# Mixer A, heads 0 to 4: 15 of 20 probability tiles transposed by VectorE in 32x32 blocks and by transfers within SBUF instead of by TensorE

## The chip, the core and the metric

The kernel is one program on one core of a Trainium2 chip. The metric is the device time in microseconds, from launch to the last write. The kernel before takes 865.27 us, the median of 3 runs (863.59 to 866.17).

## The reference

One layer of a bidirectional encoder, x of 512 tokens by 1024, float32:

```python
h = rms_norm(x)
z = h @ w_in                      # q, k, v of mixer A; q, k, v of mixer B; two gates
ya = axial_gqa_attention(qa, ka, va) @ w_o_a
yb = dilated_window_attention(qb, kb, vb) @ w_o_b
x = x + (gate_a * ya + gate_b * yb) @ w_out
x = x + expert_choice_swiglu(rms_norm(x))     # 16 experts, 64 tokens each
return rms_norm(x)
```

Mixer A has 8 query heads of 64 and 2 key heads. Per head and query block it computes s = q k^T over all 512 keys, p = softmax(s), o = p v. The change touches the way in which p gets its keys onto the partitions, so that p v can be summed over them.

## The kernel before, in words

Tokens are dealt to 4 tiles of 128: token 4 i + c lies on partition i of tile c. The kernel runs in stages on one core: norm and token-major projections; mixer A (8 heads of 4 query tiles, 32 tiles u = 4 head + c); mixer B (4 heads, 16 tiles); gates, branch projections and output projection; router; then 8 pairs of experts, whose weights stream from HBM. Each engine has its own instruction list, written out by hand, and semaphores join them. There is no planner: the order in which each engine makes its steps is the order of the loops below, and an engine that waits holds up all that stands behind it in its list.

In mixer A the lists run in turns u:

- TensorE (`for u in range(NA)`, lines 1391 on): `scores_a(u + 2)` makes two 128x512 score matmuls (L1322) into one of three PSUM banks and waits for `exp_done` of tile u-1, whose bank it takes; `values_a(i)` (L1364), at u = 9, 17 and 25 and once in mixer B, sums p v of two heads in 16 matmuls; `fill` makes one or two steps of three matmuls (L1165 to L1167) of the projections of mixer B, by the plan `A_FILL`; `turn_probs(u)` makes four 128x128 transposes (L1352) of the normalised probabilities of tile u into PSUM.
- VectorE (`for u in range(NA + 5)`): the maximum of tile u (L2010); `norm_probs(u - 1)`, a reciprocal (L1980) and a scaling of 128x512 (L1982); `low_col`, the low parts of finished q and k columns of mixer B (L1998, L2002, L2003), `split_lo` (L1887), the low part of a weight strip, in the turns `A_LOWS`; `low_o`, the low part of a pair's output, in the turns `O_LOW`.
- ScalarE (`for u in range(NA + 4)`): `soft_exp(u)` (L885), `read_probs(u - 2)` (L897), the copy of the transposed tile from PSUM into `pT`, `high_col` (L916, L919, L920), `split_hi` (L801), `read_o` in the turns `O_READ`. From head 2 on `read_probs` waits for `pv_done`, since it overwrites the `pT` that `values_a` reads.
- SyncE issues the loads of the weight strips, one DMA each, in the order of `strips`. `load_strip(n)` (L595) waits until VectorE has split strip n-4. Strips 12 to 23 are the q and k columns of mixer B.

`pT` holds two heads, `[key partition, head % 2, key tile, query]`. The probabilities lie in three rotating buffers `probs_a`; `wait_probs_free` holds an exponential until the tile three before has been transposed.

```python
for u in range(NA):
    if u + 2 < NA:
        scores_a(u + 2)
    if u > 1 and u % (2 * NT) == 1:
        values_a(u // (2 * NT) - 1)
    fill(A_FILL, u, cols_a, A_LEAD)
    turn_probs(u)
```

## Time and profile before

| | |
|---|---|
| median of 3 runs | 865.27 us (863.59 to 866.17) |
| profiled execution | span 862.3 us from the first to the last instruction; no time of its own is listed for it beside the three |
| instructions | 10445 |
| TensorE busy | 843.6 us, 98% |
| VectorE, ScalarE, GpSimd busy | 373.8, 264.2, 29.1 us |
| HBM | 235.92 MB read, 2.62 MB written |
| granted TensorE clock | 0.996 of full speed, mean |

The profile is one execution. PE is TensorE's matmul, PEld its weight load, DVE is VectorE, ACT ScalarE, POOL GpSimd, SP SyncE. L1352 is line 1352 of the kernel. Durations of neighbours on one engine overlap, so what an instruction costs is read from the distance of starts. The chain is the work that ended last, followed back from the end at each step to what released it.

### The profile page before, as it was taken

To read this page: it belongs to the slowest core of one execution; us is meant where nothing else is said; L and a number is where in the kernel's file an instruction comes from. 1 tells how busy PE (TensorE), PEld (TensorE's weight loads), DVE (VectorE), ACT (ScalarE), POOL (GpSimd) and SP (SyncE) were. 2 spreads that over 40 slices of the span, in tenths; PEclk is the share of its full clock that TensorE was granted. 3 is DMA by queue.
4 is the path that set the end of the run, shared out by engine and by line. 5 is a ranking of instruction groups with operands and counts; after the bars stand their busy time and mean duration, and the time that the engine had idled before them with its cause. 6 is when DMAs were issued, how large, how long until landed. Compare 5 with 4: busy or idle time off the path is not lost.

```text
span 862.3 us, 10445 instructions
## 1 busy us (share of the span) xinstructions
PE 843.6 (98%) x4229; PEld 517.8 (60%) x4229; DVE 373.8 (43%) x648; ACT 264.2 (31%) x461; POOL 29.1 (3%) x50
## 2 busy tenths in 40 slices
PE   9999999999999999999999999999999998989996
PEld 8898866787878888888534343344433433334343
DVE  6377987776616244427322236223131321312351
ACT  6333876685624233216011010010100101001231
POOL 1050000000000000003000000000000000000010
PEclk9999999999999999999999999999999999999999
DMA  9730112033034334884899999999999999999996
GB/s 286 177 98 2 49 49 98 25 87 97 20 122 134 92 92 143 310 369 165 333 406 424 427 431 427 427 426 429 426 427 428 428 428 427 427 424 429 425 421 256
DMA packets 81491, 239.20 MB, mean 277 GB/s; under 512 B 8102, under 2 KB 63526, under 8 KB 65828
## 3 DMA queue, kind: packets, MB, share of 16 engines
q1 hardware_dynamic: 76016, 235.94, 69.4%
q10 hardware_dynamic: 5284, 2.09, 1.0%
q8 instruction: 34, 0.56, 0.3%
q0 software_dynamic: 144, 0.51, 0.1%
q14 instruction: 13, 0.11, 0.0%
HBM read 235.92 MB, written 2.62 MB: 277 GB/s over the span
## 4 chain that ended last, share of the span: by engine, by line
PE 90%; DMA 8%; DVE 1%; issue 0%; ACT 0%; POOLq 0%; POOL 0%; SPq 0%; DVEq 0%; ACTq 0%
PE psum L1652 21%; PE psum L1165 11%; PE psum L1684 11%; PE psum L1166 11%; PE psum L1167 11%; DMA wslot<-in_w_down 8%; PE psum L1609 3%; PE psum L1703 3%; PE psum L1352 3%; PE psum L1813 2%; PE psum L1322 2%; PE psum L1364 2%; PE psum L1338 2%; PE psum L1171 1%; PE psum L1664 1%; PE psum L1617 1%
## 5 line engine op out<-in xcount | busy, mean ns | idle before, releaser
L1652 PE MATMUL psum<-wslot,xinT 128*64 128x512 f32 x1000 | 222.3, 595 | 4.6 <-DMA wslot<-in_w_up 2.8
L1652 PEld LDWEIGHTS psum<-wslot,xinT 128*64 128x64 f32 x1000 | 69.3, 137 | 142.7 <-issue 131.3
L1684 PE MATMUL psum<-wslot,actT 128*64 128x512 f32 x424 | 95.8, 596 | 3.8 <-DMA wslot<-in_w_down 3.8
L1165 PE MATMUL psum<-hT_hi,w_hi 128*128 128x512 f32 x208 | 82.9, 399 | 0.0
L1167 PE MATMUL psum<-hT_hi,w_lo 128*128 128x512 f32 x208 | 81.2, 390 | 0.0
L1166 PE MATMUL psum<-hT_lo,w_hi 128*128 128x512 f32 x208 | 81.2, 390 | 0.0
L1887 DVE TENSOR_TENSOR w_lo<-w_raw,w_hi 128x1024 fp32r<-128x1024 f32 (+1 forms) x46 | 52.9, 1175 | 44.9 <-ACT w_hi L801 44.7
L1684 PEld LDWEIGHTS psum<-wslot,actT 128*64 128x64 f32 x424 | 29.4, 137 | 59.8 <-issue 57.3
L1097 ACT ACTIVATE actT<-psum 128x512 f32<-128x512 f32 x16 | 9.6, 598 | 171.7 <-PE psum L1664 171.7
L2294 DVE TENSOR_TENSOR x<-x,psum 128x512 f32<-128x512 f32 x48 | 29.8, 682 | 57.5 <-PE psum L1703 57.5
L2284 DVE TENSOR_TENSOR y_lo<-psum,y_hi 64x512 fp32r<-64x512 f32 x28 | 19.3, 689 | 79.7 <-ACT y_hi L1107 79.3
L801 ACT ACTIVATE w_hi<-w_raw 128x1024 fp32r<-128x1024 f32 (+1 forms) x46 | 45.2, 1017 | 16.3 <-PE psum L1167 16.3
L1165 PEld LDWEIGHTS psum<-hT_hi,w_hi 128*128 128x128 f32 x208 | 39.1, 188 | 10.0 <-issue 2.6
L1167 PEld LDWEIGHTS psum<-hT_hi,w_lo 128*128 128x128 f32 x208 | 39.0, 188 | 8.4
L1166 PEld LDWEIGHTS psum<-hT_lo,w_hi 128*128 128x128 f32 x208 | 39.1, 188 | 7.5
L1092 ACT ACTIVATE act<-psum,slot_vals 128x512 f32<-128x512 f32 x16 | 11.0, 687 | 93.3 <-PE psum L1652 93.3
L2271 DVE SCALAR_TENSOR_TENSOR act<-psum,slot_vals,act 128x512 f32<-128x512 f32 x16 | 12.0, 750 | 59.1 <-ACT act L1092 59.0
L897 ACT ACTIVATE pT<-psum 128x512 f32<-128x512 f32 x48 | 28.5, 595 | 22.7 <-PE psum L1352 13.3
L1107 ACT ACTIVATE y_hi<-psum 64x512 fp32r<-64x512 f32 x28 | 16.5, 589 | 57.3 <-PE psum L1684 57.0
L1609 PE MATMUL psum<-xn,pick 128*128 128x512 f32 x120 | 29.4, 396 | 0.0
L2237 DVE TENSOR_TENSOR xinT<-psum,small 128x512 f32<-128x512 f32 x15 | 9.7, 686 | 40.0 <-PE psum L1617 40.0
L2277 DVE SCALAR_TENSOR_TENSOR act<-act,slot_fac,psum 128x512 f32<-128x512 f32 x16 | 12.0, 748 | 31.9 <-PE psum L1652 31.9
(281 smaller groups left out, 1307.7 us busy)
## 6 DMA issues: line engine op xcount, KB each, us to landing
wslot<-in_w_up SPq DMA_DIRECT2D x24, 2048.0 KB, 25.5
wslot<-in_w_gate SPq DMA_DIRECT2D x24, 2048.0 KB, 24.5
wslot<-in_w_down SPq DMA_DIRECT2D x22, 2048.0 KB, 22.5
w_raw<-in_w_in SPq DMA_DIRECT2D x34, 512.0 KB, 4.6
wslot<-in_w_up SPq DMA_DIRECT2D x15, 1024.0 KB, 10.5
wslot<-in_w_down SPq DMA_DIRECT2D x15, 1024.0 KB, 27.6
wslot<-in_w_gate SPq DMA_DIRECT2D x14, 1024.0 KB, 11.2
w_raw<-in_w_out SPq DMA_DIRECT2D x8, 512.0 KB, 4.7
```

The lines of the kernel that those rows point to most:

```text
L801: act_.activation(hi, raw, ACT.Copy).then_inc(w_hi_done, 1)
L897: last = act_.activation(pT[:, head % 2, :, cols], tp[(0, 3)[u % 2]][:, :].rearrange("p (k i) -> p k i", i=P), ACT.Copy)
L1165: pe.matmul(out_, s_hi, m_hi, start=(k == 0), stop=False)
L1166: pe.matmul(out_, s_hi, m_lo, start=False, stop=False)
L1167: return pe.matmul(out_, s_lo, m_hi, start=False, stop=(k == n_k - 1))
L1352: t = pe.transpose(tp[(0, 3)[u % 2]][:, P * k:P * k + P], probs_of(u)[:, P * k:P * k + P], ident[:, :])
L1609: mm = pe.matmul(bank[6 + f][:, :], pick[:, c, :, :], part[:, c, cols], start=(c == 0 and part is xn_hi), stop=(c == NT - 1 and part is xn ...
L1652: mm = pe.matmul(bank[2 * e + n][CAP * f:CAP * f + CAP, :], xinT[:, HALF * h + k, CAP * e:CAP * e + CAP], wslot[place_of(m)][:, k % PART, ...
L1684: mm = pe.matmul(bank[4 + e][CAP * f:CAP * f + CAP, :], actT[:, e, k, CAP * h:CAP * h + CAP], wslot[place_of(m)][:, k % PART, SEQ * f:SEQ ...
L1703: mm = pe.matmul(bank[added_bank(c, f)][:, :], give[:, p % 2, P * c:P * c + P], part[:, SEQ * f:SEQ * f + SEQ], start=(part is y_hi), stop ...
L1887: dve.tensor_tensor(lo, raw, hi.bitcast(F32), ALU.subtract).then_inc(w_split, 1)
L2294: dve.tensor_tensor(part, part, bank[added_bank(c, f)][:, :], ALU.add).then_inc(added, 1)
```

## The change

For the tiles c = 0, 1, 2 of heads 0 to 4 (`in_blocks`, 15 of the 32 tiles of mixer A) the way of the probabilities is another one:

- VectorE makes the reciprocal alone; ScalarE scales the 128x512 tile in place (`scale_probs`); VectorE transposes it in sixteen 32x32 blocks (`turn_blocks`) into one of two buffers `blocks`; when the three tiles of a head are there, SyncE issues 16 DMAs of 32 partitions by 4 by 96 numbers from `blocks` into `pT` (`move_blocks`), which carries each block to the partitions of its keys. TensorE's four transposes and ScalarE's copy out of PSUM are left out for these tiles.
- Tile c = 3 of each of these heads, and all tiles of heads 5 to 7, go as before. `whole_before(u)` counts those.
- `move_blocks(0)` to `move_blocks(4)` stand on SyncE ahead of the loads of strips 19 to 23. From head 2 on they wait for `pv_done`. A buffer of `blocks` is written again once its head has been moved.
- `values_a(0)` to `values_a(2)` stand in turns 12, 20 and 25, with `read_o` and `low_o` behind them, and wait for the transfers of their heads too.
- In `pT` the queries of heads 0 to 5 lie in another order, which `read_o` and `low_o` put right with strided patterns.
- Two pairs of load semaphores are joined into `shape_parts_in`. `high_col` waits for head 3's transfer ahead of the k column of group 1, whose place one `blocks` buffer shares.

```diff
@@ -55,6 +55,8 @@
+SQ = 32
+BLOCK_HEADS = 5
 COL_A = 0
@@ -123,6 +125,7 @@
     pT = sb("pT", [2, NT, SEQ], W0)
+    blocks = [sb(f"blocks{i}", [NT, NT, 3 * SQ], kib) for i, kib in enumerate((96, W0 + 76))]
     probs_a = [sb(f"probs_a{i}", [SEQ], W0 + 16 + 2 * i) for i in range(3)]
@@ -387,11 +392,44 @@
+        def in_blocks(u):
+            return u < NT * BLOCK_HEADS and u % NT < NT - 1
+        def whole_before(u):
+            return sum(not in_blocks(v) for v in range(u))
+        def blocks_before(u):
+            return u - whole_before(u)
+        def wait_blocks_in(eng, h):
+            eng.wait_ge(blocks_in[h % 2], 16 * NT * NT * (h // 2 + 1))
         def wait_probs_free(eng, u):
             before = u - 3 if u < NA else max(u - 3, NA - 1)
-            if before >= 0:
-                eng.wait_ge(probs_turned, before + 1)
+            if before >= 0 and in_blocks(before):
+                eng.wait_ge(blocks_turned, blocks_before(before + 1))
+            elif before >= 0:
+                eng.wait_ge(probs_turned, whole_before(before + 1))
+        def turned_bank(u):
+            return tp[(0, 3)[whole_before(u) % 2]]
+        def token_order(i, rows):
+            if i > (BLOCK_HEADS - 1) // 2:
+                return rows
+            return rows.rearrange("p (q c s) -> p c q s", q=NT, c=NT)
+        def by_tiles(i, rows):
+            if i > (BLOCK_HEADS - 1) // 2:
+                return rows
+            return rows.rearrange("p (c q s) -> p c q s", q=NT, c=NT)
@@ -471,7 +509,8 @@
         A_FILL = [min(N_COL_A * KC, A_LEAD + 2 + (i + 1) * (N_COL_A * KC - A_LEAD - 2) // (NA - 1)) for i in range(NA)]
-        O_READ, O_LOW = (10, 19, 26), (11, 21, NA)
+        VALUES_AT = (12, 20, 25)
+        O_READ, O_LOW = (14, 22, 26), (15, 23, NA)
         A_LOWS = (5, 7, 10, 16, 20, 26)
@@ -639,8 +678,21 @@
+            def move_blocks(h):
+                sp.wait_ge(blocks_turned, 3 * (h + 1))
+                if h >= 2:
+                    sp.wait_ge(pv_done, h // 2)
+                for kq in range(NT):
+                    for q in range(NT):
+                        sp.dma_start(pT[SQ * kq:SQ * kq + SQ, h % 2, :, P * q:P * q + 3 * SQ],
+                                     blocks[h % 2][SQ * q:SQ * q + SQ, :, kq, :]).then_inc(blocks_in[h % 2], 16)
             load_x(0)
             for n in range(len(strips)):
+                if 19 <= n < 19 + BLOCK_HEADS:
+                    move_blocks(n - 19)
                 load_strip(n)
@@ -893,17 +945,28 @@
                     act_.wait_ge(pv_done, head // 2)
-                act_.wait_ge(probs_turned, u + 1)
-                last = act_.activation(pT[:, head % 2, :, cols],
-                                       tp[(0, 3)[u % 2]][:, :].rearrange("p (k i) -> p k i", i=P), ACT.Copy)
+                act_.wait_ge(probs_turned, whole_before(u + 1))
+                if head <= (BLOCK_HEADS - 1) // 2 * 2 + 1:
+                    dst = pT[:, head % 2, :, :].rearrange("p k (q c s) -> p k q c s", q=NT, c=NT)[:, :, :, c, :]
+                    src = turned_bank(u)[:, :].rearrange("p (k q s) -> p k q s", k=NT, q=NT)
+                else:
+                    dst = pT[:, head % 2, :, cols]
+                    src = turned_bank(u)[:, :].rearrange("p (k i) -> p k i", i=P)
+                last = act_.activation(dst, src, ACT.Copy)
                 if u >= NA:
...
+            def scale_probs(u):
+                act_.wait_ge(probs_normed, u + 1)
+                p = probs_of(u)[:, 0:SEQ]
+                act_.activation(p, p, ACT.Copy, scale=column(rinv, u)).then_inc(probs_scaled, 1)
             def read_o(i):
                 act_.wait_ge(pv_done, i + 1)
-                act_.activation(oT_hi[:, i, :], tp[2][:, :], ACT.Copy).then_inc(o_hi_done, 1)
+                act_.activation(by_tiles(i, oT_hi[:, i, :]), token_order(i, tp[2][:, :]), ACT.Copy).then_inc(o_hi_done, 1)
@@ -916,6 +979,8 @@
                 else:
+                    if (grp, hp, hh) == (1, 0, 0):
+                        wait_blocks_in(act_, BLOCK_HEADS // 2 * 2 - 1)
                     act_.activation(kB[half, hh, grp, 0, :], src[half, :], ACT.Copy)
@@ -925,8 +990,10 @@
-                        act_.dma_start(dist[:, :, :], distance).then_inc(dist_in, 16)
-                if 2 <= u < NA + 2:
+                        act_.dma_start(dist[:, :, :], distance).then_inc(shape_parts_in, 16)
+                if u and in_blocks(u - 1):
+                    scale_probs(u - 1)
+                if 2 <= u < NA + 2 and not in_blocks(u - 2):
                     read_probs(u - 2)
@@ -1339,23 +1406,27 @@
             def turn_probs(u):
+                if in_blocks(u):
+                    return
                 pe.wait_ge(probs_normed, u + 1)
...
-                    pe.wait_ge(pT_done, u)
+                    pe.wait_ge(pT_done, whole_before(u))
                     for g in range(2):
...
                                      probs_of(u)[:, SEQ + P * g:SEQ + P * g + P], ident[:, :])
-                elif u >= 2:
-                    pe.wait_ge(pT_done, u - 1)
+                elif whole_before(u) >= 2:
+                    pe.wait_ge(pT_done, whole_before(u) - 1)
                 for k in range(NT):
-                    t = pe.transpose(tp[(0, 3)[u % 2]][:, P * k:P * k + P],
+                    t = pe.transpose(turned_bank(u)[:, P * k:P * k + P],
                                      probs_of(u)[:, P * k:P * k + P], ident[:, :])
...
-                pe.wait_ge(pT_done, 2 * NT * (i + 1))
+                pe.wait_ge(pT_done, whole_before(2 * NT * (i + 1)))
+                for h in range(2 * i, min(2 * i + 2, BLOCK_HEADS)):
+                    wait_blocks_in(pe, h)
                 if i:
@@ -1391,8 +1462,8 @@
                     scores_a(u + 2)
-                if u > 1 and u % (2 * NT) == 1:
-                    values_a(u // (2 * NT) - 1)
+                if u in VALUES_AT:
+                    values_a(VALUES_AT.index(u))
                 fill(A_FILL, u, cols_a, A_LEAD)
@@ -1977,14 +2048,27 @@
                 dve.wait_ge(exp_done, u + 1)
+                if in_blocks(u):
+                    dve.reciprocal(column(rinv, u), column(rsum, u)).then_inc(probs_normed, 1)
+                    return
                 settle(dve.reciprocal(column(rinv, u), column(rsum, u)))
...
+            def turn_blocks(u):
+                head, c = divmod(u, NT)
+                if c == 0 and head >= 2:
+                    wait_blocks_in(dve, head - 2)
+                dve.wait_ge(probs_scaled, blocks_before(u + 1))
+                dve.transpose(blocks[head % 2][:, :, :, SQ * c:SQ * c + SQ].rearrange("p k q s -> p (k q) s"),
+                              probs_of(u)[:, 0:SEQ].rearrange("p (b s) -> p b s", s=SQ)).then_inc(blocks_turned, 1)
             def low_o(i):
                 dve.wait_ge(o_hi_done, i + 1)
-                dve.tensor_tensor(oT_lo[:, i, :], tp[2][:, :], oT_hi[:, i, :].bitcast(F32), ALU.subtract)\
-                    .then_inc(o_lo_done, 1)
+                dve.tensor_tensor(by_tiles(i, oT_lo[:, i, :]), token_order(i, tp[2][:, :]),
+                                  by_tiles(i, oT_hi[:, i, :].bitcast(F32)), ALU.subtract).then_inc(o_lo_done, 1)
@@ -2011,6 +2095,8 @@
                     norm_probs(u - 1, SEQ)
+                if u >= 2 and in_blocks(u - 2):
+                    turn_blocks(u - 2)
                 for g in range(N_COL_A):
```

## Rows read from the trace of the kernel before

**Rows 1.** Page part 1: busy time, share of the span and instructions of each engine.

```profile
PE 843.6 (98%) x4229; PEld 517.8 (60%) x4229; DVE 373.8 (43%) x648; ACT 264.2 (31%) x461; POOL 29.1 (3%) x50
```

**Rows 2.** Page part 4: the chain that ended last, shares by engine.

```profile
PE 90%; DMA 8%; DVE 1%; issue 0%; ACT 0%; POOLq 0%; POOL 0%; SPq 0%; DVEq 0%; ACTq 0%
```

**Rows 3.** Stretches: length, busy time of each engine, TensorE clock, DMA share, GB/s.

```profile
88.00:111.20 23.20, 23.20 (x121) 16.92 (x119) 21.75 (x43) 17.80 (x38) 0.00 (x0) 1.00 0.16 46
111.20:163.00 51.80, 51.77 (x269) 37.80 (x268) 39.98 (x83) 38.46 (x83) 0.00 (x0) 1.00 0.22 72
500.00:600.00 100.00, 100.00 (x471) 41.69 (x471) 36.94 (x59) 10.75 (x18) 0.00 (x0) 1.00 1.01 428
```

**Rows 4.** The chain in order of time: start, length, what.

```profile
107.93 3.58 PE psum L1364 x16
...
116.99 0.44 PE psum L1352 x4
117.43 0.46 PE psum L1322 x2
```

**Rows 5.** Groups by line and form, ScalarE, 88 to 163 us.

```profile
L897 ACT ACTIVATE pT<-psum 128x512 f32<-128x512 f32 x30 | 17.8, 593 | 10.8 <-PE psum L1364 9.4 <-PE psum L1352 1.4
```

**Rows 6.** Waits, 88 to 163 us: total, times, longest.

```profile
ACT pT L897 <- PE psum L1364: 9.4, 3, 3.6
...
DVE kB L2002 <- ACT kB L920: 4.5, 3, 3.6
```

**Rows 7.** VectorE in order of time: start, duration, line, operation.

```profile
98.81 1.22 DVE L1887 TENSOR_TENSOR w_lo<-w_raw,w_hi 128x1024 fp32r<-128x1024 f32 x1
99.94 0.68 DVE L2010 TENSOR_REDUCE small<-psum 128x1 f32<-128x512 f32 x1
100.54 0.15 DVE L1980 RECIPROCAL small<-small 128x1 f32<-128x1 f32 x1
100.73 0.49 DVE L1982 TENSOR_SCALAR probs_a<-probs_a,small 128x512 f32<-128x512 f32 x1
101.13 0.68 DVE L2010 TENSOR_REDUCE small<-psum 128x1 f32<-128x512 f32 x1
...
109.96 0.68 DVE L2010 TENSOR_REDUCE small<-psum 128x1 f32<-128x512 f32 x1
```

**Rows 8.** SyncE's DMA issues in order of time, and line 583's time to landing.

```profile
350.87 1.77 SPq L657 DMA_DIRECT2D x<-in_x  x4
...
401.02 0.68 SPq L628 DMA_DIRECT2D wslot<-in_w_up  x1
...
190.07 0.51 SPq L584 DMA_DIRECT2D w_raw<-in_w_o_b  x1
...
DMA to landing us min/median/max: 2.6/2.7/3.0
```

**Rows 9.** TensorE in order of time: start, duration, line, operation.

```profile
117.73 0.40 PE L1165 MATMUL psum<-hT_hi,w_hi 128*128 128x512 f32 x1
...
119.12 0.60 PE L1352 MATMUL psum<-ident,probs_a 128*128 128x128 f32 x4
...
136.75 0.70 PE L1322 MATMUL psum<-kA,qA 128*128 128x512 f32 x2
137.29 0.40 PE L1165 MATMUL psum<-hT_hi,w_hi 128*128 128x512 f32 x1
...
147.48 3.65 PE L1364 MATMUL psum<-pT,vA 128*64 128x512 f32 x16
```

**Rows 10.** Stretches as in rows 3, at the start and the end.

```profile
5.00:10.00 5.00, 5.00 (x26) 3.53 (x25) 2.85 (x4) 3.43 (x5) 0.77 (x2) 0.90 1.13 349
854.00:855.00 1.00, 0.89 (x3) 0.06 (x1) 0.21 (x1) 0.76 (x3) 0.00 (x0) 1.00 0.08 33
...
858.00:859.00 1.00, 0.00 (x0) 0.00 (x0) 0.00 (x0) 0.00 (x0) 0.72 (x1) 0.94 0.00 0
859.00:862.30 3.30, 0.00 (x0) 0.00 (x0) 0.00 (x0) 0.00 (x0) 0.51 (x1) 0.50 0.38 154
```

More of the change, by code:

```diff
@@ L243, in encoder_block @@
         g1_spread = sem("g1_spread")
-        rope_parts_in = sem("rope_parts_in")
+        shape_parts_in = sem("shape_parts_in")
         gains_in = sem("gains_in")
         x_tile_in = [sem(f"x_tile_in{c}") for c in range(NT)]
-        dist_in = sem("dist_in")
         w_raw_in = [sem(f"w_raw_in{i}") for i in range(RING + 2)]
@@ L274, in encoder_block @@
         probs_turned = sem("probs_turned")
+        probs_scaled = sem("probs_scaled")
+        blocks_turned = sem("blocks_turned")
+        blocks_in = [sem(f"blocks_in{i}") for i in range(2)]
         pT_done = sem("pT_done")
@@ L808, in _ @@
             square_x(2)
-            act_.dma_start(rope_in[:, :, :, :], rope).then_inc(rope_parts_in, 16)
+            act_.dma_start(rope_in[:, :, :, :], rope).then_inc(shape_parts_in, 16)
             for dst, src in ((gq, q_norm_g), (gk, k_norm_g)):
-                act_.dma_start(dst[:, :], src[0].partition_broadcast(P)).then_inc(rope_parts_in, 16)
+                act_.dma_start(dst[:, :], src[0].partition_broadcast(P)).then_inc(shape_parts_in, 16)
             square_x(3)
@@ L1368, in values_b @@
             def values_b(hp):
-                pe.wait_ge(pT_done, NA + 2 * NT * (hp + 1))
+                pe.wait_ge(pT_done, whole_before(NA + 2 * NT * (hp + 1)))
                 pe.wait_ge(o_lo_done, OA + hp)
@@ L1901, in _ @@
                 split_lo(n)
-            dve.wait_ge(rope_parts_in, 16 * 3)
+            dve.wait_ge(shape_parts_in, 16 * 3)
             for n, g in enumerate((gq, gk)):
@@ L2025, in _ @@
                     low_o(O_LOW.index(u))
-            dve.wait_ge(dist_in, 16)
+            dve.wait_ge(shape_parts_in, 16 * 4)
             for hp in range(2):
```

## The prediction

> **What bounds the kernel now.** I read the busy shares first: TensorE (PE) is busy 98% of the 862.3 us span [rows 1]. The chain that ended last lies on it for 90%, with 8% on the weight loads [rows 2]. Two stretches differ by limit. Mixer A is 88 to 163 us: there TensorE is busy throughout, and in its first part VectorE nearly as much (21.75 of 23.2 us), afterwards 39.98 of 51.8; the DMA engines are used for about a fifth. Late, at 500 to 600 us, TensorE and the DMA engines are both full, but the DMA there is fed by slots that TensorE frees [rows 3]. So a microsecond won or lost in mixer A moves everything behind it by one, as long as TensorE is what runs out there.
>
> I call the 32 query tiles of mixer A u = 0 to 31 (head u // 4). In turn u TensorE makes scores(u+2), some projection steps, then the transposes of tile u. VectorE in its turn u takes the maximum of tile u and normalises u-1. scores(u+2) waits for the exponential of u-1.
>
> **TensorE.** Four transposes take 0.44 us on the chain, two score matmuls 0.46, a values_a of 16 matmuls 3.58 [rows 4]. 15 of the 20 tiles of heads 0 to 4 lose their transposes: 15 x 0.44 = 6.6 us less. That is the whole prize. values_a moves from turns 9, 17, 25 to 12, 20, 25.
>
> **ScalarE.** Each of the 15 tiles exchanges a 128x512 copy out of PSUM (593 ns, [rows 5]) for a scaling of 128x512 in SBUF. Between the copy's 593 and a little over that, I take no change. Its wait for values_a (3 times, 9.4 us in all, [rows 6]) moves with values_a and stays as long. The strided reads and writes of read_o and low_o keep their element counts, so nothing is charged; they lie off the chain.
>
> **VectorE.** Starts of neighbours give the pitch: the scaling of 512 numbers 0.40 us (100.73 to 101.13), the maximum over 512 numbers 0.60 (99.94 to 100.54), a 1024-number subtraction 1.13 (98.81 to 99.94) [rows 7]. No row shows a VectorE transpose. I bound it by 0.40 and 1.13 and take 0.60, since it passes 512 numbers once like the maximum. So each of 15 tiles adds 0.2 us, 3.0 in all. In the first part VectorE has no room: seven tiles (0, 1, 2, 4, 5, 6, 8) are turned ahead of max(11), which moves from 109.96 [rows 7] to 111.4. It also waits some 0.8 us at the first tile of head 2 for head 0's transfer to land (110.3, below, against 109.5 wanted). Then 0.6 for the maximum and some 0.7 for the exponential: scores(14) can run at about 113.5 and end at 114.0. TensorE alone would have been there near 110.
>
> **The transfers.** This term decides. Each of five heads is moved by 16 DMAs that SyncE issues one after the other, 80 in all. An issue holds SyncE: four loads in a row with no wait between them took 1.77 us (0.44 each), two others 0.68 (0.34), and one after another took 0.51 alone, so with the gap 0.55 [rows 8]. I take 0.41 per issue, and 0.34 to 0.55 as bounds. The smallest weight loads land 2.7 us after their issue (2.6 to 3.0) [rows 8]; mine are in SBUF at both ends, so 2.0 is possible. A head thus needs 15 x 0.41 + 2.7 = 8.9 us from first issue to landing and blocks SyncE for 6.6.
>
> Order on SyncE: strip 18 waits for a split that ends at 99.94 [rows 7], plus 0.6 for three transposed tiles, so it is issued at 100.65. Head 0 goes 101.1 to 107.6 (landed 110.3), strip 19 to 108.0, head 1's last DMA is issued at 108.0 + 6.15 = 114.2 and lands at 116.9. values_a(0) waits for it, with TensorE standing behind: it starts at 116.9 instead of 114.0 and ends at 120.5. Before, TensorE had reached the same place in the order (values_a(0) made, projection steps of turn 12 next) at 117.73 [rows 9]. So it is 2.8 us late there already.
>
> Heads 2 and 3 overwrite what values_a(0) reads, so SyncE waits for it, then issues 32 DMAs and two strips: 120.5 + 6.6 + 0.4 + 6.15 + 2.7 = 136.3, and values_a(1) can end at 139.9. VectorE gives a second bound for the same place. Tile 19 is still transposed by TensorE, and its normalising stands behind, from max(15) at 120.5 + 1.4 + 0.5 = 122.4: six maxima 3.6, six reciprocals 1.1, four transposes 2.4, two scalings 0.8, one low_o 0.7, one split 1.1, four 64x512 subtractions of the k column 2.8, which is 12.5; and for ScalarE's k copies about 1.5 (such waits cost 4.5 us now, [rows 6]). That makes 136.4, transposes and scores 0.9, values_a(1) 3.6: 140.9. Before, that place was reached at 137.29 [rows 9]. Both paths say late, by 2.6 and 3.6. I take +3.7 with the small SyncE waits.
>
> Head 4 goes after values_a(1): 140.9 + 15 x 0.41 + 2.7 = 149.8. TensorE needs 10.2 us from there to values_a(2) (137.29 to 147.48, [rows 9]), so until 151.1: hidden by 1.3 us, and by less than nothing if an issue costs 0.55. The strips that now stand behind transfers (19 to 23) are needed turns later, the last in mixer B: no cost while the queue is free by 150. ScalarE's wait before the k column of group 1 is for head 3, landed long before. The freed semaphore and the shared count cost nothing.
>
> A rule of the Trainium skill speaks otherwise about the main term. The rows show 0.34 to 0.55 us for one issue [rows 8]. The page "DMA: Bandwidth & Descriptors", section "Anatomy of one DMA — SWDGE (gpsimd) path", puts the sequencer's dispatch of a DMA at about 50 ns; if that held on SyncE here, 16 issues would be an estimated 0.8 us and the transfers would be hidden. That is rival B below; the rows do not bear it out.
>
> **Sum.** -6.6 of TensorE work, +10.3 of waits (the two values_a and tile 19), so +3.7: span 862.3 to 866.0. The profiled execution's span lies 3.0 under the median of 865.27, so on that scale the forecast is 865.3 + 3.7 = 869.0. About 0.3% (2.6 us) is what a measurement of this kernel can tell from no change.
>
> **Rivals.**
> A, the forecast: SyncE's issues and VectorE's chain hold both values_a back. With issues of 0.34 the transfers would allow 135.5, but VectorE's chain, from a values_a(0) ending at 118.3, still 138.7 (+1.4); with 0.55, values_a(1) ends at 113.7 + 64 x 0.55 = 148.9, and head 4 adds 0.8: +12.4. Its own range is 866.7 to 877.7. For it: nothing on SyncE between issues explains the 0.4 but the issue itself. Chance 0.45.
> B, issues are cheap and transfers hidden, VectorE alone limits: values_a(0) starts at 114.0, VectorE's chain then gives 117.6 + 1.9 + 12.5 + 4.5 = 136.5 and up to 1.5 of waiting for ScalarE, so within 1 us of the old 137.29, 865.3. For it: VectorE is at 94% in the first part [rows 3]. Chance 0.22; that the change does nothing to the chain at all is another 0.02 at the same time.
> C, the other side: a VectorE transpose costs about 0.40, the same as the scaling it replaces, and an issue less than 0.33. The transfers let values_a(1) end at 113.7 + 64 x issue, which equals the old 137.29 at 0.37 and is 2.6 better at 0.33; below that VectorE decides: max(11) stays at 109.96, values_a(0) ends at 111.8 + 3.6 = 115.4, then 1.9 + 11.7 + 1.1 and 4.5 as above, 134.6. So -2.7: 862.6, and never better than -6.6, 858.7. Against it: no issue in the trace is under 0.33. Chance 0.16.
> D, A plus the clock. TensorE would stand idle about 3 us before values_a(0) and 3.4 before tile 19's transposes. At the end of the kernel it stops at 854.9, and the granted clock is 0.94 in 858 to 859 and 0.50 after, i.e. 1.2 instead of 2.4 GHz; after an early fall 5 to 10 us shows 0.90 [rows 10]. A fall that lasts as long as the one row of 3.3 us at half clock costs 1.7 us of work; two make 872.4. No row shows an idle of 3 us within the kernel, so it is open. Chance 0.07.
> E, a transpose costs 1.13: VectorE adds 0.5 to each of seven tiles first and four later, the start of values_a(0) moves to 117.7 and the second chain by 2.1, so about +6.5, 871.8. Chance 0.08.
>
> **How the numbers follow.** A, D and E are slower by over 0.3%: 0.60. B and nothing: 0.24. C: 0.16, its time on the edge of 0.3% and beyond. The predicted time is A's, 869.0. The range 862.0 to 878.0 takes in B, the near half of C and A's upper bound; A's own stands above.
>
> **What would show it.** The SyncE rows of the new DMAs: a pitch of 0.4 us makes 6.6 us a head. TensorE's waits: matmuls of values_a released by a DMA, about 3 us for the first, and its start near 117 instead of 107.9. Tile 19's transposes released by VectorE, 3 us idle. The VectorE transpose at 0.6 us pitch (duration about 0.69). values_a(1) ending near 141 against 131.5, and the projection step behind it near 141 against 137.29; mixer B beginning 3.7 us late and everything behind it shifted by the same. Wrong would be: issues of 0.1 us, no idle before values_a, or a shift that is made up before 163 us.

## The result, and the profile after

| | before | after |
|---|---|---|
| median of 4 runs each | 864.43 us (862.91 to 866.17) | 893.50 us (892.86 to 894.07) |
| ratio | | 1.0335, 95% interval 1.0317 to 1.0353 |
| profiled execution | span 862.3 us | 893.24 us, span 891.3 us |
| mean granted TensorE clock | 0.996 | 0.976 |

The kernel is 29 us slower. The forecast was 869.0 us with a range of 862 to 878: the direction was right, the size was not, and it lies outside the range. Some executions of the kernels here, the one before included, take about 2.5 us more than the others, and where a trace shows this it is there before 60 us, ahead of the change.

The page of the changed kernel, its parts 1, 2 and 4. It answers to [rows 1] and [rows 2]:

```profile
PE 846.7 (95%) x4169; PEld 515.5 (58%) x4169; DVE 375.7 (42%) x648; ACT 265.9 (30%) x461; POOL 29.0 (3%) x50
...
PEclk9999967899999999999999999999999999999998
...
PE 82%; DMA 8%; SPq 5%; DVE 2%; issue 2%; ACT 1%; POOLq 0%; POOL 0%; DVEq 0%; ACTq 0%
```

TensorE fell from 98% busy to 95%, and its share of the chain from 90% to 82%. SyncE's queue (SPq), which was not on the chain, holds 5% of it. The granted clock drops in slices 6 to 8 of 40, which is mixer A.

Where the time went is seen by comparing the two kernels at the same places in TensorE's order:

| place in TensorE's order | before | after | later by |
|---|---|---|---|
| projection steps of turn 12, values_a(0) made | 117.73 | 129.66 | 11.9 |
| projection steps of turn 20, values_a(1) made | 137.29 | 159.59 | 22.3 |
| values_a(2) begins, turn 25 | 147.48 | 175.89 | 28.4 |
| mixer B's first scores | 163.15 | 193.31 | 30.2 |
| end of the span | 862.3 | 891.3 | 29.0 |

All of it is lost between 105 and 193 us; 1 us comes back behind, in stages that were not changed. The stretches, answering to [rows 3]; columns are the window, busy us and count of PE, PEld, DVE, ACT and POOL, then the granted clock, the DMA share and GB/s:

```profile
88.00:111.20 23.20, 20.61 (x92) 15.95 (x91) 19.41 (x37) 19.45 (x40) 0.00 (x0) 1.00 0.20 53
111.20:130.00 18.80, 9.25 (x28) 3.92 (x28) 7.64 (x15) 4.50 (x11) 0.00 (x0) 0.64 0.39 104
130.00:150.00 20.00, 14.27 (x60) 10.49 (x58) 15.48 (x28) 14.47 (x29) 0.00 (x0) 0.88 0.39 96
150.00:170.00 20.00, 16.86 (x70) 10.19 (x70) 8.98 (x22) 9.85 (x22) 0.00 (x0) 0.77 0.37 106
170.00:190.00 20.00, 14.11 (x62) 8.95 (x63) 9.48 (x18) 7.23 (x16) 0.00 (x0) 0.83 0.33 75
190.00:210.00 20.00, 20.00 (x120) 15.19 (x120) 14.76 (x34) 14.13 (x30) 0.00 (x0) 1.00 0.00 1
```

From 111 to 130 us TensorE works for half of the time, VectorE for 41% and ScalarE for 24%: nobody is busy, so something outside of the three is waited for. The waits between 88 and 195 us name it (total, times, longest):

```profile
DVE small L2094 <- PE psum L1389: 21.5, 4, 10.3
...
PEld psum L1421 <- DVE probs_a L2056: 13.8, 6, 4.9
PE psum L1421 <- DVE probs_a L2056: 11.3, 5, 4.4
DVE blocks L2065 <- DMA pT<-blocks: 10.0, 3, 4.2
PE psum L1435 <- DMA pT<-blocks: 8.4, 2, 5.2
```

L2094 is the maximum, L2056 the scaling on VectorE, L2065 the new transposes, L1435 `values_a`, L1421 TensorE's transposes, L1389 the scores. Two engines wait for the transfers into `pT` directly: TensorE in `values_a`, and VectorE, which may not overwrite a `blocks` buffer before it has been moved. The rest are echoes: VectorE's normalising of tiles 11 and 19 stands behind its own wait, TensorE's transposes stand behind that, and VectorE's maximum in turn waits for scores that stand behind TensorE.

SyncE's timeline shows the cause. Columns are start, busy us, queue and line, what, and how many:

```profile
100.33 0.37 SPq L634 DMA_DIRECT2D w_raw<-in_w_in  x1
100.75 10.39 SPq L689 DMA_DIRECT2D pT<-blocks  x16
111.18 0.59 SPq L634 DMA_DIRECT2D w_raw<-in_w_in  x1
111.81 10.60 SPq L689 DMA_DIRECT2D pT<-blocks  x16
122.46 0.59 SPq L634 DMA_DIRECT2D w_raw<-in_w_in  x1
129.83 10.26 SPq L689 DMA_DIRECT2D pT<-blocks  x16
140.13 0.59 SPq L634 DMA_DIRECT2D w_raw<-in_w_in  x1
140.84 10.61 SPq L689 DMA_DIRECT2D pT<-blocks  x16
151.49 0.59 SPq L634 DMA_DIRECT2D w_raw<-in_w_in  x1
159.74 11.08 SPq L689 DMA_DIRECT2D pT<-blocks  x16
```

Sixteen issues hold the queue for 10.4 us: 10.39 / 16 = 0.65 us each, not 0.41 (the five heads: 0.64 to 0.69). Heads 0 and 1 take SyncE from 100.75 to 122.41 without a gap worth the name, heads 2 and 3 from 129.83 to 151.45. Head 2 can only start when `values_a(0)` has ended, and head 4 when `values_a(1)` has.

TensorE's timeline shows what that does. In brackets is the idle time before, and what ended it:

```profile
105.43 0.66 PE L1421 MATMUL psum<-ident,probs_a 128*128 128x128 f32 x4 [1.15 <-DVE probs_a L2056]
...
116.82 1.11 PE L1421 MATMUL psum<-ident,probs_a 128*128 128x128 f32 x4 [4.39 <-DVE probs_a L2056]
...
123.94 5.80 PE L1435 MATMUL psum<-pT,vA 128*64 128x512 f32 x16 [5.16 <-DMA pT<-blocks]
...
147.81 1.11 PE L1421 MATMUL psum<-ident,probs_a 128*128 128x128 f32 x4 [4.44 <-DVE probs_a L2056]
...
153.07 6.59 PE L1435 MATMUL psum<-pT,vA 128*64 128x512 f32 x16 [3.29 <-DMA pT<-blocks]
...
175.89 5.42 PE L1435 MATMUL psum<-pT,vA 128*64 128x512 f32 x16 [5.96 <-issue]
```

Five idles of 3.3 to 6.0 us make 23.2 us. Behind each one the next matmuls take longer: 1.11 instead of 0.66 us for four transposes, 5.4 to 6.6 instead of 3.65 us for a `values_a`. The granted clock was at the lower level (0.50, 1.2 instead of 2.4 GHz) for the stretch 115.5 to 118.7, and between 0.56 and 0.68 on average around each of the three `values_a`. Before, no clock below 1.00 shows in mixer A.

### The profile page after: what moved, and what is told of

Read it like the earlier page. It is cut to its first block, busy times and chain, and to the rows that moved or that the text cites. A ratio compares the mean times of both kernels' runs of the same rounds, so it can differ in the third digit from the quotient of the medians.

```text
span 891.3 us, 10390 instructions
## 1 busy us (share of the span) xinstructions
PE 846.7 (95%) x4169; PEld 515.5 (58%) x4169; DVE 375.7 (42%) x648; ACT 265.9 (30%) x461; POOL 29.0 (3%) x50
## 3 DMA queue, kind: packets, MB, share of 16 engines
HBM read 235.92 MB, written 2.62 MB: 268 GB/s over the span
## 4 chain that ended last, share of the span: by engine, by line
PE 82%; DMA 8%; SPq 5%; DVE 2%; issue 2%; ACT 1%; POOLq 0%; POOL 0%; DVEq 0%; ACTq 0%
PE psum L1723 20%; PE psum L1755 11%; PE psum L1232 10%; PE psum L1234 10%; PE psum L1233 10%; DMA wslot<-in_w_down 7%; SPq L689 4%; PE psum L1680 3%; PE psum L1774 3%; PE psum L1435 2%; PE psum L1884 2%; PE psum L1405 2%; PE psum L1421 1%; PE psum L1735 1%; PE psum L1238 1%
## 5 line engine op out<-in xcount | busy, mean ns | idle before, releaser
L1435 PE MATMUL psum<-pT,vA 128*64 128x512 f32 x64 | 21.5, 832 | 14.4 <-DMA pT<-blocks 8.4
L955 ACT ACTIVATE pT<-psum 128x512 f32<-128x512 f32 x33 | 19.6, 596 | 43.8 <-PE psum L1435 30.7
L2094 DVE TENSOR_REDUCE small<-psum 128x1 f32<-128x512 f32 x32 | 21.7, 681 | 21.9 <-PE psum L1389 21.5
## 6 DMA issues: line engine op xcount, KB each, us to landing
wslot<-in_w_gate SPq DMA_DIRECT2D x24, 2048.0 KB, 23.3
```

The lines of the kernel that those rows point to most:

```text
L1435: mm = pe.matmul(tp[2][HD * hh:HD * hh + HD, :], vA[:, k, HD * kv:HD * kv + HD], pT[:, hh, k, :], start=(k == 0), stop=(k == NT - 1))
```

## The experiments

Two theories stood before these runs. **I**: SyncE's issue of a transfer, 0.65 us, is the cause, and all stalls follow from it. **V**: VectorE's longer chain is. Beside them: the transfers' traffic, the strips that now come late, the clock, and the `blocks` buffers. In some kernels part of the transposed probabilities is left out; where that is so the expectation says it. In these GpSimd also sets `pT` to zero, and SyncE and ScalarE wait for that; in the one-transfer trace it is done at 87.2 us, ahead of mixer A. The cuts of code show the main lines of an edit.

**One transfer per head.** The other fifteen are dropped:

```diff
-                for kq in range(NT):
-                    for q in range(NT):
+                for kq, q in [(kq, q) for kq in range(NT) for q in range(NT)][:1]:
```

> The changed kernel with 1 of each head's 16 transfers (15/16 of the blocks of heads 0 to 4 stay away from pT, which is set to zero first). Theory I, SyncE's issues at 0.645 us each hold both values_a back: the delay goes with the transfers, values_a(0) starts near 114 instead of 123.9, no idle is long, the clock stays at 1.00 and the time is 862 to 867 us. Rival V, VectorE's chain with its 0.62 us transposes is enough to make it slow: 868 us or more, with values_a(1) ending over 3 us later than the 131.5 plus the turns it was moved by, i.e. the projection step behind it past 141.

Measured: 868.27 us, 7 runs, ratio 1.0058 (1.0039 to 1.0078). Of the 29 us, 25 go with the fifteen transfers that were dropped, but 4 remain, so neither theory has it alone. Its TensorE timeline (`values_a` is L1438 here, the transposes L1424):

```profile
114.37 3.65 PE L1438 MATMUL psum<-pT,vA 128*64 128x512 f32 x16
...
134.98 0.66 PE L1424 MATMUL psum<-ident,probs_a 128*128 128x128 f32 x4 [3.34 <-DVE probs_a L2059]
136.04 5.32 PE L1438 MATMUL psum<-pT,vA 128*64 128x512 f32 x16
```

`values_a` has no wait before it any more. Tile 19's transposes still wait 3.3 us for VectorE, and the clock falls there once: it is 0.68 of full speed on average during values_a(1), which takes 5.32 us instead of 3.65. values_a(1) ends at 141.36; before it was at 131.5 in its old turn, and the place behind it was reached at 137.29. So 4.1 us late at that place, which is all of the +4.2; 1.7 of it is the low clock, and 2.4 are left for VectorE's chain.

**Four and eight transfers per head**, the same edit with `[:4]` and `[:8]`.

> Each head is moved by 4 of its 16 transfers from SyncE's queue; the other blocks are left out (zero). Theory I: 2.6 us of SyncE a head, hidden behind VectorE's chain, which alone gives 868.3 with one transfer: 868 to 869.5. A rival by which the cost grows evenly with the number of issues (25.2 us over 15 issues, so 1.7 us per issue and head) gives 868.3 + 3 x 1.7 = 873.3.

> Each head is moved by 8 of its 16 transfers, all from SyncE's queue; the other blocks of the transposed probabilities are left out (they are zero), so the output is not the reference's. Theory I (SyncE's issues decide, 0.64 us each): a head blocks SyncE for 5.2 us, as in two_queues, where 8 of 16 came from SyncE, so the time is that of two_queues, 871 us, between 869 and 873, and values_a(0) has its blocks by about 114.5. Rival T (it is the transfers' number or bytes in flight that decide, whoever issues them): two_queues moved twice the bytes, so eight_moves would be clearly faster than it, near one_move's 868.3.

Measured: 868.62 us with eight (7 runs, ratio 1.0051, 1.0035 to 1.0068), and with four 871.85, 871.77 and 868.10 us. SyncE's rows, of eight and then of four:

```profile
100.55 5.24 SPq L689 DMA_DIRECT2D pT<-blocks  x8
106.51 5.10 SPq L689 DMA_DIRECT2D pT<-blocks  x8
```

```profile
103.05 2.67 SPq L689 DMA_DIRECT2D pT<-blocks  x4
108.30 2.52 SPq L689 DMA_DIRECT2D pT<-blocks  x4
```

The four-transfer execution, of 871.85 us, was already 2.5 us late before its first transfer (103.05 against 100.55). GpSimd's rows show the same distance at 54 us (51.65 in the one-transfer trace, 54.09 here), ahead of everything that was edited. Without it, it would lie near 869.3; about 1.1 us more is between tile 19 and the end of values_a(1), where the clock fell four transposes earlier. With three runs, two of them at 871.8 and one at 868.10, four's own time is known only to some 3 us. One and eight transfers cost the same, 868.3 and 868.6, and sixteen cost 893.5: between them is a threshold, not a slope. Eight a head are issued by 111.6, so even with 2 us on top the last has landed at 113.6, before `values_a(0)` is wanted at 114.3; in its trace `values_a(0)` waits for nothing. An even slope of 1.7 us per issue would have made 880 of eight and is out, though 873 for four lies within 1.5 us of two of its three runs. For eight, I had put down 871, the two-queue kernel's time, and that was 2.4 too much; the eight-transfer trace equals the one-transfer trace within 0.2 us up to values_a(2). By the letter of the expectation, 868.6 is what rival T said. The next run limits T: it moves all sixteen, so their number and bytes can be worth at most the 2.4 us by which it lies above eight.

**Two queues.** All sixteen transfers, the blocks of the upper two key tiles' partitions issued from GpSimd:

```diff
 SyncE:
-                for kq in range(NT):
+                for kq in range(NT // 2):
 GpSimd:
+            for h in range(BLOCK_HEADS):
+                pool.wait_ge(blocks_turned, 3 * (h + 1))
...
+                for kq in range(NT // 2, NT):
+                    for q in range(NT):
+                        pool.dma_start(pT[SQ * kq:SQ * kq + SQ, h % 2, :, P * q:P * q + 3 * SQ],
+                                       blocks[h % 2][SQ * q:SQ * q + SQ, :, kq, :]).then_inc(rows_written, 16)
```

> Half of each head's 16 transfers issued by GpSimd's queue, idle in mixer A, half by SyncE. Theory I, the issues of one queue in a row (0.645 us each) set the landing of a head: SyncE needs 5.2 us a head, and if GpSimd's pitch is no longer than 1 us the head lands 3 to 5 us earlier, values_a(0) starts by 120 and the time is below 882 us, at best 868 to 872 as with one transfer per head. Rival: the DMA engines or a part shared by both queues paces the transfers: no less than 890 us.

Measured: 871.00 us (870.36 to 874.26, 3 runs), ratio 1.0082 (1.0053 to 1.0112), with all of the work done. The issues of heads 0 and 1 on GpSimd's queue, head 0's on SyncE's, and TensorE's rows:

```profile
97.55 4.65 POOL L796 DMA_DIRECT2D pT<-blocks  x8 [34.13 <-DVE blocks L2076]
106.06 4.33 POOL L796 DMA_DIRECT2D pT<-blocks  x8 [3.86 <-DVE blocks L2076]
```

```profile
100.44 5.27 SPq L690 DMA_DIRECT2D pT<-blocks  x8
```

```profile
114.26 3.65 PE L1446 MATMUL psum<-pT,vA 128*64 128x512 f32 x16
...
134.88 1.12 PE L1432 MATMUL psum<-ident,probs_a 128*128 128x128 f32 x4 [3.34 <-DVE probs_a L2067]
136.78 5.74 PE L1446 MATMUL psum<-pT,vA 128*64 128x512 f32 x16
```

The same 80 transfers with the same bytes, issued from two queues instead of one, take 22.5 us off, and `values_a(0)` starts as if there were a single transfer. It is the issue that costs, on the queue that makes it. Of the 1.9 us of span by which this execution lies above eight transfers, 1.3 appear from tile 19 to the end of values_a(1), where the clock fell four transposes earlier (1.12 against 0.66 us); the rest comes behind mixer A. The page "DMA: Bandwidth & Descriptors" of the Trainium skill, section "Issuing engines are not separate DMA queues", says that issuing from several engines only saves the sequencer's time for the issue, which it calls usually small relative to the DMA. The first half agrees with this run. The second doesn't hold here: a transfer lands 2.0 us after its issue (median in the changed kernel), and the issue is 0.65 of it.

**Short transfers.** Sixteen per head, each with one of its four runs of 384 B per partition:

```diff
-                        sp.dma_start(pT[SQ * kq:SQ * kq + SQ, h % 2, :, P * q:P * q + 3 * SQ],
-                                     blocks[h % 2][SQ * q:SQ * q + SQ, :, kq, :]).then_inc(blocks_in[h % 2], 16)
+                        sp.dma_start(pT[SQ * kq:SQ * kq + SQ, h % 2, 0:1, P * q:P * q + 3 * SQ],
+                                     blocks[h % 2][SQ * q:SQ * q + SQ, 0:1, kq, :]).then_inc(blocks_in[h % 2], 16)
```

> 16 transfers per head, but each carries one run of 384 bytes per partition instead of four (3/4 of the blocks of heads 0 to 4 stay away from pT, which is set to zero first). Theory I in its form that an issue costs the same whatever it carries: the pitch stays 0.6 to 0.65 us and the time 890 to 895. Rival S, an issue is priced by the number of its runs (128 against 32): the pitch falls to about 0.4 and the time to 872 to 878.

Measured: 891.18 us (2 runs), ratio 1.031 (1.0274 to 1.0346). Its SyncE row:

```profile
103.17 10.09 SPq L690 DMA_DIRECT2D pT<-blocks  x16
```

A quarter of the bytes and of the runs, and an issue still costs 10.09 / 16 = 0.63 us. What an issue carries hardly counts; that it is one does. The median is 2.3 us below the changed kernel's, with two runs against four.

**Transfers alone.** The kernel before, with 48 transfers of the same form that nobody needs, ahead of strips 19 to 21:

```diff
             for n in range(len(strips)):
+                if 19 <= n < 22:
+                    move_spare(n - 19)
                 load_strip(n)
```

> The kernel before plus 48 transfers of the same shape (three heads' worth) on SyncE ahead of strips 19 to 21, from hT_hi into unused memory; nobody waits for them but the k column of group 1. If only the waits for the transfers cost: no change, 863 to 866 us, with a pitch of 0.6 to 0.65 us between issues. If the traffic itself or the strips that stand behind it cost: 867 us or more.

Measured: 864.47 us (10 runs), ratio 1.0001 (0.9985 to 1.0016).

```profile
100.22 11.26 SPq L649 DMA_DIRECT2D spare<-hT_hi  x16
112.84 10.27 SPq L649 DMA_DIRECT2D spare<-hT_hi  x16
124.52 10.95 SPq L649 DMA_DIRECT2D spare<-hT_hi  x16
```

SyncE is held as long as by three heads of the changed kernel, strips 19 and 20 come as late (issued at 111.53 and 123.16, there 111.18 and 122.46), and it costs nothing. So what these heads cost is neither their traffic nor the strips, but that somebody waits for the last of the sixteen. Heads 3 and 4 and the strips behind them are not in this run, and head 4 is another matter (see the last run).

**A third buffer**, dealt to the heads as 0, 1, 2, 1, 0, so that VectorE needn't wait for heads 0 and 2 to be moved:

```diff
-    blocks = [sb(f"blocks{i}", [NT, NT, 3 * SQ], kib) for i, kib in enumerate((96, W0 + 76))]
+    blocks = [sb(f"blocks{i}", [NT, NT, 3 * SQ], kib) for i, kib in enumerate((96, W0 + 76, W0 + 88))]
...
-                if c == 0 and head >= 2:
+                if c == 0 and head >= 3:
```

> The changed kernel with a third blocks buffer, so that VectorE's transposes of heads 2 and 4 don't wait for heads 0 and 2 to be moved. Rival B, these waits (10.0 us of VectorE, with 4.4 us of TensorE idle behind each of tiles 11 and 19) are a cost of their own: both idles go, 884 to 886 us. Theory I, the landing of heads 1 and 3 holds values_a anyway: the idle moves into the wait of values_a, 891 to 894 us.

Measured: 894.99 us (2 runs), ratio 1.0349 (1.0309 to 1.0389). In the changed kernel VectorE's wait looks like a cause of its own, with 10.0 us. Here it is gone at tile 11, and `values_a(0)` waits 8.95 us instead of 5.16:

```profile
126.07 5.64 PE L1437 MATMUL psum<-pT,vA 128*64 128x512 f32 x16 [8.95 <-DMA pT<-blocks]
```

The wait moved, the time stayed: it had been hidden behind the transfers. From head 0's first issue to `values_a(0)` it is 22.8 us here (from 103.23) and 23.2 in the changed kernel (from 100.75). At tile 19 VectorE still keeps TensorE waiting, 3.3 us instead of 4.4.

**Transfers one strip earlier**, ahead of strips 18 to 22:

```diff
-                if 19 <= n < 19 + BLOCK_HEADS:
-                    move_blocks(n - 19)
+                if 18 <= n < 18 + BLOCK_HEADS:
+                    move_blocks(n - 18)
```

> Each head's transfers one strip earlier in SyncE's list, so head 0's need not wait for the split of strip 14. Theory I: SyncE starts at about 97.6 instead of 100.75, values_a(0) starts 3.1 us earlier, at 120.8, and all behind it moves by as much: 890 to 891 us. If VectorE's chain or the clock set the place instead: 893 to 894.

Measured: 890.13 us (2 runs), ratio 1.0292 (1.0257 to 1.0328); `values_a(0)` starts at 120.75 instead of 123.94. The start of the queue is worth its 3 us once, and no more, because heads 2 to 4 start when `values_a` lets them.

**Clock.** Dummy matmuls in TensorE's idle times, so that it never stands still:

```diff
+                if u in (11, 19):
+                    pe.wait_ge(pT_done, whole_before(u) - 1)
+                    keep_clock(20, turned_bank(u))
                 pe.wait_ge(probs_normed, u + 1)
...
+                if i < OA - 1:
+                    if i:
+                        pe.wait_ge(o_lo_done, i)
+                    keep_clock(30, tp[2])
                 pe.wait_ge(pT_done, whole_before(2 * NT * (i + 1)))
```

> The changed kernel with 20 small matmuls ahead of the waits of tiles 11 and 19 and 30 ahead of the waits of values_a(0), (1) and (2), all inside TensorE's idle time. If the clock's fall is a cost of its own: granted clock 1.00 through mixer A, each values_a back from 5.8, 6.6 and 5.4 us to 3.6, so 7.0 us less, 886 to 887 us. If the transfers cover it: the clock stays up but the time stays within 1.5 us of 893.5.

Measured: 892.12 us (4 runs), ratio 1.0325 (1.0295 to 1.0354). The clock was 1.00 in all of mixer A and the three `values_a` took 3.65 us each, but some dummies outlasted the wait that they filled. Hence a second one with fewer: 16 ahead of tiles 11 and 19, and 22, 16 and 6 ahead of the three `values_a`.

> As the run with small matmuls in the idle time, but fewer of them (16 for tiles 11 and 19; 22, 16 and 6 for values_a(0), (1), (2), of 0.23 us each), since 30 outlasted the waits by 0.6, 2.1 and 4.3 us. If the clock's fall has a price on the chain, the three values_a win 2.1, 2.9 and 1.8 us: 886 to 888 us. If the transfers cover it: 892 to 894.

Measured: 892.40 us (4 runs, 890.57 to 895.38), ratio 1.033 (1.0294 to 1.0366). TensorE's rows, then SyncE's for head 2:

```profile
123.87 3.65 PE L1442 MATMUL psum<-pT,vA 128*64 128x512 f32 x16 [1.39 <-DMA pT<-blocks]
...
152.00 3.65 PE L1442 MATMUL psum<-pT,vA 128*64 128x512 f32 x16 [0.56 <-DMA pT<-blocks]
...
171.95 6.19 PE L1442 MATMUL psum<-pT,vA 128*64 128x512 f32 x16 [4.68 <-issue]
```

```profile
127.62 11.42 SPq L689 DMA_DIRECT2D pT<-blocks  x16
```

`values_a(1)` began only 1.1 us earlier than in the changed kernel although `values_a(0)` took 2.15 us less: head 2's sixteen issues began 2.2 us earlier but took 11.42 us instead of 10.26. At the end of values_a(1) this execution is 4.0 us ahead, and then values_a(2), behind 4.68 us of idle, fell to the low clock all the same (6.19 us). Mixer B's first scores come 3.1 and 3.2 us earlier than in the changed kernel in the two clock kernels, the profiled spans are 1.6 and 2.7 us below its 891.3, the medians 1.4 and 1.1 below. So the low clock is real in the trace, and filling the idle time gave back 1 to 3 us, not the 6.9 by which the three `values_a` are longer. But neither run is a clean price: one has dummies that outlast the waits, the other a third `values_a` at the low clock, and the runs spread over 5 us. What the clock costs in full stays open.

**Half of the transpose.** One transfer per head, and VectorE turns 256 of the 512 columns:

```diff
-                              probs_of(u)[:, 0:SEQ].rearrange("p (b s) -> p b s", s=SQ)).then_inc(blocks_turned, 1)
+                              probs_of(u)[:, 0:SEQ // 2].rearrange("p (b s) -> p b s", s=SQ)).then_inc(blocks_turned, 1)
```

> one_move with VectorE transposing only the first 256 of 512 key columns (the rest left out, zero in the output's sum). Theory V (the +4.2 us of one_move are VectorE's chain): 15 transposes shorter by about 0.3 us, 7 of them ahead of max(11) and 4 between values_a(0) and tile 19, so 1 to 3 us less than one_move's 868.3: 865 to 867.5, and tile 19's wait of 3.3 us shrinks to about 2. Rival: VectorE's pace is not the cause (ScalarE's scaling of 0.71 us instead of the copy of 0.59, and its reads, are): 868.3 again and tile 19's wait stays above 3.

Measured: 867.46 us (10 runs), ratio 1.0033 (1.0020 to 1.0045); the profiled span is 863.6 against 865.9 with whole transposes. Two rows, TensorE's and VectorE's:

```profile
112.59 3.65 PE L1438 MATMUL psum<-pT,vA 128*64 128x512 f32 x16
...
132.88 1.12 PE L1424 MATMUL psum<-ident,probs_a 128*128 128x128 f32 x4 [3.28 <-DVE probs_a L2059]
```

```profile
117.54 0.69 DVE L2085 SCALAR_TENSOR_TENSOR qB<-psum,qB 64x512 fp32r<-64x512 f32 x1 [3.15 <-ACT qB L982]
```

`values_a(0)` comes 1.8 us earlier: in the first part the time is VectorE's. From there to tile 19 it takes 20.3 us against 20.6, and the wait is 3.28 where it was 3.34, though four transposes there are some 0.27 us shorter each. VectorE's idle times grew instead: it waits 3.15 us (2.62 with whole transposes) for ScalarE's q column, and ScalarE stands behind `values_a(0)`. From the start of `values_a(0)` to that q column of VectorE it is 4.95 us in both kernels. So the second part reads as a chain of VectorE, ScalarE and TensorE handing on to one another, and not as VectorE's work alone; no run isolates its members. The expectation of a wait of about 2 was wrong there, and the rival's wait of more than 3 came in. The median fell by only 0.8 us where the spans fell by 2.3; the profiled run is the fastest of its ten (865.64 of 865.64 to 868.36), so the size of the gain is loosely known.

**Head 0 alone**, to see if any dose pays: `BLOCK_HEADS = 1`, `values_a` in turns 10, 17 and 25, transfers ahead of strip 18.

> The change for head 0 alone (3 of 32 tiles, 16 transfers), values_a kept at turns 10, 17 and 25, transfers ahead of strip 18. Theory: TensorE saves 3 x 0.44 = 1.3 us; VectorE's three transposes add 3 x 0.2 us before max(11), 16 issues hold SyncE for 10.4 us from about 100 and land by 112.5, while values_a at turn 10 is wanted near 109.5. So the saving is given back: 864 to 867 us, no change by 0.3%. If VectorE's chain and the issues had cover here, 863.1 would be seen.

Measured: 865.02 us (12 runs), ratio 1.0004 (0.9990 to 1.0018). `values_a(1)`, in its old turn, starts at 128.43, before at 127.88: 0.55 us late. TensorE waits 0.90 and 0.97 us for VectorE ahead of two of its transposes, together more than the 1.3 us saved. No kernel with the change in it was faster than the kernel before.

**dist later.** The third stall was longer than the issues explain: head 4's last transfer was issued at 170.2, and with a landing of 2.0 us `values_a(2)` could have begun at 172.3. It began at 175.89. At 166.1 ScalarE issues the 1536 KB load of `dist` in its turn 24. The changed kernel's row for head 4's transfers, and for those of the heads before:

```profile
DMA to landing us min/median/max: 1.9/2.6/7.1
...
DMA to landing us min/median/max: 1.9/2.0/3.7
```

```diff
-                    if u == 3 * NA // 4:
+                    if u == 27:
                         act_.dma_start(dist[:, :, :], distance).then_inc(shape_parts_in, 16)
```

> The changed kernel with one edit: ScalarE issues the 1536 KB load of dist in turn 27 instead of 24, so behind the turn of values_a(2). In the changed kernel head 4's sixteen transfers are issued from 159.7 to 170.2 us and land up to 7.1 us later, where those of the heads before land within 3.7, and dist is issued at 166.1; TensorE waits 5.96 us until 175.89. Theory L (the last transfers queue behind dist on the DMA engines): without it the last one, issued at 170.2, lands 2.0 to 3.0 us later, values_a(2) starts at 172.3 to 173.3, its wait is 2.4 to 3.4 us, the largest landing falls below 4 us, and the time falls by 2.6 to 3.6 us to about 890 to 891. dist is then on its way before mixer B wants it at 196 and costs nothing. Rival Q (SyncE's own issues and the wait for values_a(1) set the start, dist beside them is harmless, as the spare transfers were harmless to the kernel before): 175.9 again and 893.5.

Measured: 890.04 us (4 runs), ratio 1.0299 (1.0274 to 1.0323), 3.5 us less than the changed kernel.

```profile
172.26 5.35 PE L1435 MATMUL psum<-pT,vA 128*64 128x512 f32 x16 [2.57 <-issue]
```

Theory L came in at its numbers: the wait 2.57 us, the longest landing of head 4's transfers 3.2 us, the time 3.5 less. In the kernel before `dist` is issued at 144.2, where the DMA engines had been busy for 12% of the 4 us before; the lateness of head 4 made the two meet.

## Why the prediction was wrong in size, step by step

**The step that failed** is "I take 0.41 per issue, and 0.34 to 0.55 as bounds". An issue of these transfers measured 0.65 us. The bounds were read past a row that breaks them. The prediction has "two others 0.68 (0.34)"; the only such row in [rows 8], at 401.02, says x1: one issue that held SyncE for 0.68 us. So a price above 0.55 was on the table before the result, and A's own range should have reached past 113.7 + 64 x 0.68 = 157.2 for the end of values_a(1), 20 us late. Besides, all rows there are loads from HBM over 128 partitions, not this form. I had written that below the range it would be cheap (rival B, rival C) and kept no case above it. The figure of the Trainium skill, page "DMA: Bandwidth & Descriptors", section "Anatomy of one DMA — SWDGE (gpsimd) path", about 50 ns for a dispatch, is 13 times too low if it is taken as the price of an issue on SyncE. On GpSimd's queue, the path that section is about, an issue took 0.54 to 0.58 us (run with two queues). Rival B is out twice: the issues are not cheap, and with one transfer per head, where they are hidden, the kernel is 4 us slower, not within 1.

**The formula carries about 20 of the 29 us.** The prediction's end of values_a(1), 113.7 + 64 x issue, gives 155.0 us with 0.645, which is 17.7 late; head 4 by the same price adds 15 x 0.645 + 2.7 - 10.2, about 2.2. That is +19.9, an estimate of 885 us. The rest are two terms that the sum did not have. One is the clock, which stood only in rival D: the three `values_a` took 6.9 us longer, and two of them stand in the path between the transfers of one pair of heads and the next. The other is the load of `dist`, 3.4 us. Against them, the transfers landed in 2.0 us and not in 2.7. `values_a(1)` began at 153.07, and with 3.65 us of work would have ended at 156.7; it ended at 159.6 at the low clock. The three places:

- Head 1 has landed at 123.9 instead of 116.9: the first stall of `values_a(0)`, and ahead of it tile 11. I had put VectorE's wait for head 0's move at 0.8 us; it was 3.38, and its normalising of tile 11 behind it kept TensorE idle for 4.4. `values_a(0)` then took 5.80 us. Place: +11.9 where I had +2.8.
- Heads 2 and 3 take 21.6 us of SyncE behind `values_a(0)`, and values_a(1) takes 6.59: +22.3 where I had +3.7.
- "Head 4 ... hidden by 1.3 us" became 5.96 us of idle. From head 4's first issue to its last it is 10.5 us (159.7 to 170.2), with a landing of 2.0 12.5, against 10.3 of TensorE work (159.59 to 169.93): some 2.3 us, which is what the run with `dist` later shows (2.57). The other 3.4 are the collision with the load of `dist`, for which the prediction had no step at all.

**VectorE.** The pitch of a transpose was taken as 0.60 and is 0.62 (112.50 to the low part of the strip at 113.14 is 0.64, 113.18 to 113.81 in the one-transfer kernel 0.63), busy 702 ns. Rival E, 1.13, is out. With one transfer per head, which leaves VectorE's chain alone, `values_a(0)` began at 114.37; the forecast without transfers was 114.0, and that had 0.8 us in it for a transfer that VectorE no longer waits for. `values_a(1)` ended at 141.36. That looks like the forecast's 140.9, and +4.2 like its +3.7, but it is luck: the 140.9 start from a `values_a(0)` that ends at 120.5, and here it ended at 118.0. From that end to the end of values_a(1) the forecast had 20.4 us, and it took 23.3. Of the 2.9 between them 1.7 are the low clock in values_a(1), 0.9 lie between the maximum of tile 15 (120.11) and tile 19's transposes (134.98), where the sum had 14.0 us. So VectorE's path was too cheap in the sum as well, which without transfers (rival B) had put the kernel within 1 us of the old time.

**TensorE** lost 15 x 0.44 = 6.6 us of transposes as said. Its total of busy time rose all the same, 843.6 to 846.7 us, because matmuls at 1.2 GHz count for longer.

**ScalarE.** "I take no change" for the scaling against the copy: the scaling takes 714 ns, the copy 592, so each tile costs ScalarE some 0.12 us more, 1.8 us over fifteen. VectorE waited for a scaling only once, for 0.4 us; no run isolates it.

**The clock, rival D.** It had 0.07, and the clock did fall, at five places. The idles were 3.3 to 6.0 us long. In the one-transfer kernel, with one such fall, 1.7 us of the +4.2 are the clock's. In the changed kernel the two clock kernels gave back 1 to 3 us, and the full price stays open between that and the 6.9 us by which the `values_a` are longer.

**What cost nothing** as said: the strips behind the first transfers and the traffic of three heads, by the run with transfers alone. For strips 21 to 23 and the joined semaphore no trace shows TensorE waiting, but no run isolates them. The traffic of head 4 was not free, as the meeting with `dist` shows.

## What to carry to other kernels

Sixteen small transfers are first of all sixteen issues on one queue: count them, take a price per issue from a row of the same form, or keep the upper bound open if there is none, and see who waits for the last one. Read the count at the end of a row before dividing by it: here an x1 read as two hid the price that came. Where nobody waits they are free (864.47 us with 48 of them); where somebody does, up to a threshold they are hidden, and beyond it they count: eight a head make 868.6, sixteen 893.5. No run lies between these two, so where the threshold is and that each issue beyond it counts in full is worked out and not shown. And an engine that is made late meets other traffic than before: look at what is issued in the microseconds into which a transfer slides.

## What the runs showed of the hardware that was not expected

- An issue on SyncE of a transfer within SBUF (32 partitions) held its queue for 0.64 to 0.69 us in the changed kernel's five sets of sixteen, and for 0.63 with a quarter of the 48 KB and of the 128 runs. Single sets in other runs were slower: 11.42 us with dummy matmuls beside them, 0.71 each.
- The same issue on GpSimd's queue took 4.65 / 8 = 0.58 us, for head 1 4.33 / 8 = 0.54. Neither queue's issues slowed the other's (head 1's eight on SyncE, beside GpSimd's, 5.15 us; without them 5.10), but the transfers landed later: a median of 2.6 and 2.8 us instead of 2.0.
- A strip load issued right behind the transfers held SyncE for 0.59 us, one behind an empty queue 0.37.
- 48 KB within SBUF landed 2.0 us after its issue (median), 1.9 to 3.7 for the heads without a large load beside them; beside a load of 1536 KB up to 7.1.
- A 128x512 fp32 transpose in 32x32 blocks took VectorE 702 ns busy; with half the columns 420 to 450 ns.
